# Gate products of a recurrence: three one-pass products of high and low parts in place of one fp32 product

## The reference

```python
xblk = xc.reshape(B, L, N_LRU_BLOCKS, LRU_BLOCK)          # 8 blocks of 128 features
r = sigmoid(einsum('blni,nij->blnj', xblk, w_rg_a) + b_rg_a)
i = sigmoid(einsum('blni,nij->blnj', xblk, w_rg_x) + b_rg_x)
log_a = -RG_C * r * softplus(-lru_lambda)
a = exp(log_a)
u = sqrt(-expm1(2.0 * log_a)) * (i * xc)
h_t = a_t * h_{t-1} + u_t                                  # scan over tokens
y = h * gelu(gl)
```

## Time and profile before

| what | value |
|---|---|
| median of 3 runs | 2026.47 us (2026.41 to 3343.63) |
| profiled execution, its own time | 2027.95 us |
| its span, first to last instruction | 2026.1 us |
| mean granted TensorE clock | 0.997 |
| busy: PE, PEld, DVE, ACT, POOL | 99%, 93%, 57%, 42%, 9% |

### The profile page before, as it was taken

The page is one execution under the profiler, slowest core; times in us unless marked ns, Lnnn a source line. Parts: engine busy times, 40 slices in busy tenths (PEclk is TensorE's granted clock), DMA queues, the critical chain, the costliest instruction groups (busy, mean ns, idle before and its releaser), DMA issues. The chain is left out here.

```text
span 2026.1 us, 35096 instructions
## 1 busy us (share of the span) xinstructions
PE 2001.9 (99%) x14624; PEld 1890.5 (93%) x14624; DVE 1158.3 (57%) x1814; ACT 849.0 (42%) x1151; POOL 182.9 (9%) x217
## 2 busy tenths in 40 slices
PE   6999999999999999999999999999999999999998
PEld 3869999999998999999988799999999999999998
DVE  5625566775446674646464355767735367646463
ACT  4124544665324244444431354446642333526252
POOL 0001020000022100000220011100000410000004
PEclk9999999999999999999999999999999999999999
DMA  9522243222254232323621314422222622322222
GB/s 361 187 73 100 82 164 104 84 81 76 83 202 161 74 126 94 133 78 134 264 74 63 115 58 135 141 89 81 82 83 77 255 70 84 103 69 101 84 88 105
DMA packets 79067, 233.91 MB, mean 115 GB/s; under 512 B 7376, under 2 KB 27856, under 8 KB 78544
## 3 DMA queue, kind: packets, MB, share of 16 engines
q1 hardware_dynamic: 57312, 206.99, 29.2%
q10 hardware_dynamic: 21616, 24.93, 3.8%
HBM read 219.80 MB, written 12.09 MB: 114 GB/s over the span
## 5 line engine op out<-in xcount | busy, mean ns | idle before, releaser
L1732 PE MATMUL acc<-h_hi,weight_h 128*128 128x288 f32 x1920 | 567.4, 298 | 0.0
L1732 PE MATMUL acc<-h_hi,weight_l 128*128 128x288 f32 x1920 | 560.3, 295 | 0.0
L1732 PE MATMUL acc<-h_lo,weight_h 128*128 128x288 f32 x1920 | 560.2, 294 | 0.0
L504 ACT ACTIVATE weight_h<-raw 128x1024 fp32r<-128x1024 f32 x188 | 199.1, 1059 | 618.0 <-PE acc L1732 515.7
L1732 PE MATMUL acc<-b_hi,weight_l 128*128 128x288 f32 x1520 | 429.5, 295 | 0.0
L1732 PE MATMUL acc<-b_hi,weight_h 128*128 128x288 f32 x1520 | 429.4, 295 | 0.0
L1732 PEld LDWEIGHTS acc<-h_hi,weight_h 128*128 128x128 f32 x1920 | 358.7, 188 | 5.3 <-issue 3.4
L1732 PEld LDWEIGHTS acc<-h_lo,weight_h 128*128 128x128 f32 x1920 | 358.5, 188 | 0.8
L1732 PEld LDWEIGHTS acc<-h_hi,weight_l 128*128 128x128 f32 x1920 | 358.3, 188 | 0.0
L1063 DVE TENSOR_TENSOR weight_l<-raw,weight_h 128x1024 fp32r<-128x1024 f32 x176 | 227.3, 1291 | 227.9 <-ACT weight_h L504 227.4
L1732 PE MATMUL acc<-b_lo,weight_h 128*128 128x288 f32 x1264 | 356.5, 294 | 0.0
(11 more groups left out here) (294 smaller groups left out, 3120.1 us busy)
## 6 DMA issues: line engine op xcount, KB each, us to landing
raw<-stream SPq DMA_DIRECT2D x290, 512.0 KB, 3.5
ada_raw<-ada_in SPq DMA_DIRECT2D x48, 512.0 KB, 6.3
first_raw<-ada_in SPq DMA_DIRECT2D x36, 512.0 KB, 14.4
s_s<-state_in ACTq DMA_DIRECT2D x8, 1024.0 KB, 6.9
ret_s_out<-s_s ACTq DMA_DIRECT2D x8, 1024.0 KB, 4.4
two_raw<-ada_in SPq DMA_DIRECT2D x12, 512.0 KB, 11.2
tables<-const_in SPq DMA_DIRECT2D x2, 1246.0 KB, 12.5
x<-x_in ACTq DMA_DIRECT2D x1, 2304.0 KB, 13.2
```

The source lines that it names most:

```text
L504: A(weight_h[:, j % 2, :], raw[:, (j + 2) % 4, :], ACT.Copy).then_inc(h_split, 1)
L1732: last = M(acc[j % 2][:, half, 0:HALF], w, r[:, k, half * HALF:(half + 1) * HALF], start=(k == order[0] and n == 0), stop=(k == order[-1] ...
```

## The change

The gate products are made in three one-pass products as the stream tiles are. The high part of the branch row and of the gate weights is rounded by ACT (`round_gate`), the low part subtracted by DVE (`split_gate`), into slots 2 and 3 of `weight_h` and `weight_l` in turn (576 columns of input, 256 of weights). PE's gates(m) waits for the split and runs 12 matmuls. The semaphores of the sample parts are merged to make room for the new ones.

Where the new steps stand: on ACT round_gate(0) in front of gate_tanh(0), round_gate(m+1) behind decay(m); on DVE split_gate(0) in front of gated_input(0), which is behind the convolution of m = 7, and split_gate(m+1) behind root_argument(m), in front of the evacuation into `mix`.

```diff
+                def round_gate(m):
+                    lm = lay * 8 + m
+                    act.wait_ge(conv_kept, lm + 1 + 1)
+                    act.wait_ge(wrg_loaded[m % 2], lay * 64 + 16 * (m // 2 + 1))
+                    if m < 2:
+                        act.wait_ge(s_update_ready, lay * 8 + 8)
+                    else:
+                        act.wait_ge(gates_ready, lm - 1)
+                    A(gate_input(weight_h, m).rearrange("p (a b) -> p a b", a=2), one(qk, m), ACT.Copy)
+                    A(gate_weight(weight_h, m), wrg[:, m % 2, :], ACT.Copy).then_inc(gate_rounded, 1)
...
+                round_gate(0)
                 gate_tanh(0)
                 for m in range(KT):
                     split_h(lay, AT_GL, 0, 2 * m)
                     gelu_square(m)
                     decay(m)
+                    if m < KT - 1:
+                        round_gate(m + 1)
                     split_h(lay, AT_GL, 0, 2 * m + 1)
...
+                def split_gate(m):
+                    lm = lay * 8 + m
+                    dve.wait_ge(gate_rounded, lm + 1)
+                    V.tensor_tensor(gate_input(weight_l, m), qk[:, m, :], gate_input(weight_h, m).bitcast(F32), ALU.subtract)
+                    V.tensor_tensor(gate_weight(weight_l, m), wrg[:, m % 2, :], gate_weight(weight_h, m).bitcast(F32), ALU.subtract).then_inc(gate_split, 1)
...
+                split_gate(0)
                 gated_input(0)
                 for m in range(KT):
                     split_l(lay, AT_GL, 0, 2 * m)
                     gelu_inner(m)
                     root_argument(m)
+                    if m < KT - 1:
+                        split_gate(m + 1)
                     done(lay, AT_GL, 0, 2 * m + 1)
...
                 def sample_updates(n, first, v_cols):
-                    pe.wait_ge(kd_split, n + 1)
-                    pe.wait_ge(v_s_split, lay * 2 + 2)
+                    pe.wait_ge(sample_split, lay * 6 + 2 + n % 4 + 1)
...
                 def gates(m):
                     n = lay * 8 + m
-                    pe.wait_ge(conv_kept, n + 1 + 1)
-                    pe.wait_ge(wrg_loaded[m % 2], lay * 64 + 16 * (m // 2 + 1))
+                    pe.wait_ge(gate_split, n + 1)
                     pe.wait_ge(gates_read, n + 1)
+                    w_hi, w_lo = (gate_weight(w, m) for w in (weight_h, weight_l))
+                    i_hi, i_lo = (gate_input(w, m) for w in (weight_h, weight_l))
                     for gate in range(2):
                         for half in range(2):
-                            last = M(misc[:, 2 * gate + half, 0:HALF], wrg[:, m % 2, gate * 128:(gate + 1) * 128], qk[:, m, half * HALF:(half + 1) * HALF],
-                                     start=True, stop=True)
+                            for c, (w, r) in enumerate(((w_hi, i_hi), (w_hi, i_lo), (w_lo, i_hi))):
+                                last = M(misc[:, 2 * gate + half, 0:HALF], w[:, gate * 128:(gate + 1) * 128], r[:, half * HALF:(half + 1) * HALF],
+                                         start=(c == 0), stop=(c == 2))
```

More of the change, by code:

```diff
@@ L302, in build @@
         y_done, y_rest, stored, waited = sem("y_done"), sem("y_rest"), sem("stored"), sem("waited")
-        kd_rounded, kd_split, v_s_rounded, v_s_split = sem("kd_rounded"), sem("kd_split"), sem("v_s_rounded"), sem("v_s_split")
+        sample_rounded, sample_split = sem("sample_rounded"), sem("sample_split")
+        gate_rounded, gate_split = sem("gate_rounded"), sem("gate_split")
         product_done, unit_high, unit_low, sums_ready = sem("product_done"), sem("unit_high"), sem("unit_low"), sem("sums_ready")
@@ L389, in build, with gate_input, gate_weight @@
         kd_hi, kd_lo = (w[0:NB_S, 3, 0:DB // 2 * DK].rearrange("p (b d) -> p b d", d=DK) for w in (weight_h, weight_l))
+        def gate_input(tile, m):
+            return tile[:, 2 + m % 2, 0:TOK]
+        def gate_weight(tile, m):
+            return tile[:, 2 + m % 2, TOK:TOK + 256]
         def lru_rows(m):
@@ L1166, in _ @@
                         dve.wait_ge(v_ready, lay * 2 + half + 1)
-                        V.tensor_copy(v_s_hi[:, cols], v_half).then_inc(v_s_rounded, 1)
-                        dve.wait_ge(v_s_rounded, lay * 2 + half + 1)
-                        V.tensor_tensor(v_s_lo[:, cols], v_half, v_s_hi[:, cols].bitcast(F32), ALU.subtract).then_inc(v_s_split, 1)
+                        V.tensor_copy(v_s_hi[:, cols], v_half).then_inc(sample_rounded, 1)
+                        dve.wait_ge(sample_rounded, lay * 6 + half + 1)
+                        V.tensor_tensor(v_s_lo[:, cols], v_half, v_s_hi[:, cols].bitcast(F32), ALU.subtract).then_inc(sample_split, 1)
                     split_l(lay, AT_V, 0, j)
@@ L1224, in _ @@
                                 dve.wait_ge(s_update_ready, n * 2)
-                            V.tensor_copy(kd_hi, kd_s[0:NB_S]).then_inc(kd_rounded, 1)
-                            dve.wait_ge(kd_rounded, n + 1)
-                            V.tensor_tensor(kd_lo, kd_s[0:NB_S], kd_hi.bitcast(F32), ALU.subtract).then_inc(kd_split, 1)
+                            V.tensor_copy(kd_hi, kd_s[0:NB_S]).then_inc(sample_rounded, 1)
+                            dve.wait_ge(sample_rounded, lay * 6 + 2 + h + 1)
+                            V.tensor_tensor(kd_lo, kd_s[0:NB_S], kd_hi.bitcast(F32), ALU.subtract).then_inc(sample_split, 1)
                             if m > 3:
```

## The result

The changed kernel takes 2043.08 us (median of 6 runs), the kernel before 2026.88 in the same runs: a ratio of 1.008, interval [1.0066, 1.0094]. It is slower by 16.2 us. The prediction said 2042.5 us, +16.0. (One of the six runs of the kernel before took 3343.63 us; comparisons leave it out.)

A forecast was written before the change was run, and what follows sets the result against it. PE was taken to bound the kernel, busy 2001.9 of 2026.1 us. Per layer -2.9 + 6.9 + 1.6 + 0.4 + 2.0 = +8.0 us, both layers +16.0, so 2042.5 us; range 2036 to 2049.

The forecast's parts named there:

- products, 16 steps: PE's gate products: 12 one-pass matmuls in 1.58 us instead of fp32 ones in 1.94, gaining 0.36 us per step.
- wait at step 0: Before each layer's first gates step: PE waits for split_gate(0), queued behind the convolution of m = 7; +6.9 us per layer.
- wait at step 1: Before each layer's second gates step: split_gate(1) stands behind root_argument(0), delayed by a 1.28 us table load; +1.6 us per layer.
- steps 2 to 7: Later gates steps, without a table load: PE stalls 0.07 us in each of six, +0.4 us per layer.
- clock: After the step 0 pause: PE restarts at 1.2 GHz for about 4.1 us, +2.0 us per layer, ends nothing to 3.3.
- sum: Whole kernel: +8.0 us per layer, +16.0 for both, giving a median of 2042.5 us, 0.8% slower.
- The rival in which the clock stays up: At the step 0 pause: the clock does not fall; +12.0 us, 2038.5; chance 0.15.
- The stated ends, +12.5 to +21: Whole kernel: the forecast's own ends, from clock 0.8 to 3.3, steps 2 to 7 at 0 to 0.3, products 0.3 to 0.4.
- it does not fall at every step: Judges the rival that the clock falls at all 16 gates steps, even short stalls: +44 us, 2070.5; chance 0.03.
- No table load was added: Judges the rival of a 1.28 us ACT table load in every gates step: 2060.5; chance 0.05 including other stalls.
- that rival: At step 0: PE finds its operands early, so no first stall; -1.8 us, 2024.7; chance 0.03.

The follow-up runs named there:

- all steps ahead: Changed kernel with split parts of steps 0 and 1 made in stage XL, those of 2 to 7 one place earlier: 2021.49 us, 0.9971.
- with the waits kept: Changed kernel with its copies, subtractions and waits, but the four fp32 matmuls of the kernel before as gate products: 2049.34 us, 1.0112.
- step 0 early: Changed kernel with the high and low parts for gates step 0 of each layer made in stage XL, at its third tile's end: 2024.86 us, 0.9991.
- step 1 early: Changed kernel with the parts for gates steps 0 and 1 of each layer made in stage XL: 2022.24 us, 0.9977.
- second profile: Profile of the changed kernel run once more, unaltered: 2043.28 us, 1.0081.
- pause filled: Changed kernel with 48 extra one-pass matmuls on PE in each layer before its wait for the split of step 0: 2039.64 us, 1.0062.
- the half-filled pause: Changed kernel with 24 extra one-pass matmuls on PE in each layer before its wait for the split of step 0: 2043.18 us, 1.0081.
- one with 36 matmuls: Changed kernel with 36 extra one-pass matmuls on PE in each layer before its wait for the split of step 0: 2040.68 us, 1.0066.

## Why the prediction was right

Term by term, with the run that tests each. Products, steps 2 to 7 and the clock are read from the starts of the matmuls, since 1.94 - 1.58 is the forecast's own figure.

| term (us) | forecast, both layers | in the traces | tested by |
|---|---|---|---|
| products, 16 steps | -5.8 | -5.4, all steps ahead | -5.4 to -5.7, and -6.3 with the waits kept |
| wait at step 0 | +13.8 | 2 x 6.95 = +13.9 | with the clock +18.2, step 0 early |
| wait at step 1 | +3.2 | 2 x 1.44 = +2.9 | +2.6, step 1 early |
| steps 2 to 7 | +0.8 | 12 x 0.05 = +0.6 | +0.75, all steps ahead (not clear of noise) |
| clock | +4.0 | 1.6 + 2.8 = +4.4, second profile 2.0 + 1.5 = +3.5 | +3.6, pause filled |
| sum | +16.0 | +16.4, with the second profile's clock +15.5 | +16.2 |

The measured span grew by 15.7. The changed kernel's profile is 0.8 us ahead on entering the stage (the last XL matmul of layer 0 starts at 351.66 against 352.47), so from there on it is 16.5 us longer. That lead doesn't come from the change: the same matmul starts between 351.2 and 352.7 us in the eleven profiles, and at 352.5 or later only in the three in which the clock fell after 39 us in the first norm (the kernel before, all steps ahead, the filled pause).

**The products.** The row of twelve like matmuls elsewhere in the kernel was right to 0.02 us: a group without a wait takes 1.59 or 1.60. What a step gains was put too high, at 0.36: it is 0.34 or 0.35 in most steps and 0.19 in the first of a layer, 5.4 us in all from the last XL matmul of layer 0 to the end. The Trainium skill's formula for an isolated matmul (TensorE: Matmul & The Clock Gate, Back-to-back issue gap) gives an estimate of 122.5 ns, and that is not what this stream does: 1.59 us for 12 is 0.132 each.

**Step 0.** That PE needed nothing recent for gates(0), and that the new split stands behind a convolution that waits for PE's last tile, was all in the order of the queues and two timestamps. The sum of the operations that the trace showed, plus 1.10 for the split, gave 6.9 against 6.95.

**Step 1 and the rest.** The table load of m = 0 was the cause that the forecast named for the second wait, and the steps without it lose only 0.05; no run takes the load away. The 1.6 was a little high, since I counted from the weight load's start; from the matmul's own start it was 1.5.

**The clock** was the one term with wide ends, nothing to 3.3 us per layer. That it falls at the long pauses was right. The 2.0 us per layer was partly luck: it took the 4.1 us from restart to rise of another place in the kernel, and the four restarts in the two profiles of the change had 3.4, 6.0, 4.3 and 3.1. The forecast of 3 to 5 us at half speed missed one of them. The rival in which the clock stays up (2038.5) is near what the filled pause gave, 2039.6. The rule of the Trainium skill (TensorE: Matmul & The Clock Gate, Why this matters for your kernels), that idle gaps between bursts of matmuls put the array back to the lower clock, agrees with these traces: the granted clock was 0.50 behind each of the pauses of 6.95 us.

**The sum.** That 16.0 and 16.2 lie so close is partly luck as well: the products were off by +0.4 us, steps 1 and 2 to 7 by -0.3 and -0.2, which nearly cancel, and the clock's share moves by 0.9 us between two profiles of the same kernel. The stated ends, +12.5 to +21, don't follow from the ends of the terms: these add up to +12.2 and to +19.4, or to +22.4 if the 0.3 us of steps 2 to 7 are meant for each step. The measured time is well inside all of them.

**The other rivals.** The clock did not fall behind the waits of 1.17 us, nor in steps 2 to 7, so it does not fall at every step. No table load was added: there are 97 in both profiles, and ACT's copies run straight behind the exponential. The first stall was there; with step 0 made early it went, and the time, 2024.86 us, is what that rival gave for this case (2024.7).

## What to carry to other kernels

When a faster form of an operation needs its operands prepared by other engines, price it by where the preparation lands in their queues: here 16 steps gained 5.4 us, and one step in each layer lost more than three times that, 18.3 with the clock, because it had next to nothing between the preparation and its use. Make the parts where the preparing engines idle, for the first step in the stage before, and the gain is there. If a long wait can't be removed, count the clock behind it as well; filling the pause in part may bring nothing.

## What was not expected of the hardware

What the clock costs is not set by the length of the pause. Behind equal pauses of 6.95 us the slow stretch of work was 3.4 us in one layer and 6.0 in the other, and 4.3 and 3.1 in the second profile of the same kernel; pauses shortened to 3.6 us of idle time cost as much in total (2043.18 against 2043.28 us); and of two pauses with 2.05 us of idle time one was followed by half speed and the other was not. What decides between them stays open. The profiles have nine pauses at step 0 with half speed behind them (two each in both profiles of the change, the waits without the gain and the half-filled pause, one with 36 matmuls), and each cost 1.5 to 2.8 us. So such a pause is to be forecast with a range, down to nothing for a short one, and not with a number.
